# Column sums of the conditioning weights in four strips, on a fused two-layer encoder kernel

## The reference

```
m = silu(c) @ ada_w[layer, sub] + ada_b[layer, sub]        # 2048 x 6144 weights
shift, scale, gate = split(m, 3)
h = x * (1 + scale) + shift
x = layer_norm(ALPHA * x + (1 + gate) * sublayer(h))
```

## Time and profile before

| | |
|---|---|
| median of three runs | 2767.97 us (2763.74 to 2770.62) |
| profiled execution | 2772.19 us |
| its span | 2770.4 us |
| TensorE busy | 2607.1 us, 94% |
| VectorE busy | 1879.7 us, 68% |
| ScalarE busy | 1204.8 us, 43% |
| granted clock of TensorE, mean | 0.972 |
| data moved | 635 MB, 229 GB/s |

### The profile page before, as it was taken

The page is one execution under the profiler, slowest core; times in us unless marked ns, Lnnn a source line. Parts: engine busy times, 40 slices in busy tenths (PEclk is TensorE's granted clock), DMA queues, the critical chain, the costliest instruction groups (busy, mean ns, idle before and its releaser), DMA issues.

```text
span 2770.4 us, 43302 instructions
## 1 busy us (share of the span) xinstructions
PE 2607.1 (94%) x17220; PEld 2083.4 (75%) x17220; DVE 1879.7 (68%) x1946; ACT 1204.8 (43%) x1036; POOL 107.3 (4%) x154
## 2 busy tenths in 40 slices
PE   6989999977898999999999987699999999999998
PEld 2348888834586888888888862388778888888886
DVE  6876656668856776777777769767756666555555
ACT  4463333345535333343444455743443334344444
POOL 1012000000002000000000011000020000000000
PEclk9999999999999999999999988899999999999999
DMA  8898888822544887887878848778657777455552
GB/s 250 337 328 283 282 263 281 290 66 77 184 152 141 271 285 260 286 273 273 277 268 282 285 166 168 274 242 285 233 174 231 238 237 238 171 183 194 176 189 76
DMA packets 245356, 635.12 MB, mean 229 GB/s; under 512 B 33186, under 2 KB 34852, under 8 KB 240900
## 3 DMA queue, kind: packets, MB, share of 16 engines
q1 hardware_dynamic: 232548, 579.27, 63.0%
q0 software_dynamic: 9536, 34.48, 4.0%
q10 hardware_dynamic: 3168, 19.92, 1.8%
HBM read 613.83 MB, written 19.79 MB: 229 GB/s over the span
## 4 chain that ended last, share of the span: by engine, by line
PE 84%; DVE 7%; ACT 3%; DMA 3%; issue 2%; SPq 0%; DVEq 0%; ACTq 0%
PE PS L270 48%; PE PS L274 24%; PE PS L223 4%; DMA araw<-in_ada_w 2%; PE PS L444 1%; ACT Pb L1089 1%; PE PS L187 1%; PE PS L1011 1%; DVE wlo L260 1%; PE PS L712 1%; PE PS L985 1%; DMA acc<-in_ada_w 1%; PE PS L699 1%; ACT H L1089 1%; DVE X L1608 1%
## 5 line engine op out<-in xcount | busy, mean ns | idle before, releaser
L270 PE MATMUL PS<-H,whi 128*128 128x512 f32 x5888 | 1865.1, 398 | 27.0 <-DVE wlo L260 19.6
L260 DVE TENSOR_TENSOR wlo<-raw,whi 128x2048 fp32r<-128x2048 f32 x368 | 843.6, 2293 | 697.1 <-ACT whi L256 696.2
L274 PEld LDWEIGHTS PS<-H,wlo 128*128 128x128 f32 x5888 | 1113.4, 189 | 262.6
L256 ACT ACTIVATE whi<-raw 128x2048 fp32r<-128x2048 f32 x368 | 705.0, 1917 | 1225.8 <-PE PS L270 1210.2
L274 PE MATMUL PS<-H,wlo 128*128 128x256 f32 x5888 | 1162.2, 279 | 0.0
L270 PEld LDWEIGHTS PS<-H,whi 128*128 128x128 f32 x5888 | 904.2, 190 | 32.3 <-DVE wlo L260 26.0
L179 DVE SCALAR_TENSOR_TENSOR acc<-araw,cact,acc 128x1024 f32<-128x1024 f32 x240 | 307.6, 1282 | 1.4 <-DMA araw<-in_ada_w 1.0
L1089 ACT ACTIVATE Pb<-PS 128x1024 f32 (+5 forms) x106 | 106.4, 1010 | 91.7 <-PE PS L712 52.1
L1652 DVE TENSOR_TENSOR H<-Pb,H 128x512 fp32r<-128x512 f32 x128 | 87.7, 685 | 0.0
L1089 ACT ACTIVATE H<-Pb 128x512 fp32r (+2 forms) x131 | 82.3, 628 | 6.2 <-DVEq L1930 6.2
L1537 DVE TENSOR_TENSOR raw<-Pb,HF 128x1024 f32<-128x1024 f32 x64 | 74.1, 1221 | 12.0 <-DMA omat<-WF 9.4
(11 more groups left out here) (299 smaller groups left out, 1381.0 us busy)
## 6 DMA issues: line engine op xcount, KB each, us to landing
raw<-in_mlp_w SPq DMA_DIRECT2D x256, 1024.0 KB, 6.0
araw<-in_ada_w SPq DMA_DIRECT2D x274, 512.0 KB, 4.6
raw<-in_mix_w_in SPq DMA_DIRECT2D x64, 1024.0 KB, 7.7
raw<-in_s_w_glu SPq DMA_DIRECT2D x32, 1024.0 KB, 7.3
acc<-in_ada_w SPq DMA_DIRECT2D x40, 512.0 KB, 8.2
raw<-in_ada_w POOLq DMA_DIRECT2D x32, 512.0 KB, 4.1
raw<-in_mix_w_out SPq DMA_DIRECT2D x16, 1024.0 KB, 5.1
vmat<-Pb ACTq DMA_DIRECT2D x8, 1024.0 KB, 7.4
```

Of the source, the lines that this page charges most:

```text
L256: nc.scalar.activation(whi[:, s % 2, :], raw[:, s, :], ACT.Copy).then_inc(S("hi_done"), 1)
L260: nc.vector.tensor_tensor(wlo[:, s % 2, :], raw[:, s, :], whi[:, s % 2, :].bitcast(F), ALU.subtract).then_inc(S("lo_done"), 1)
L270: return nc.tensor.matmul(PS[:, b, :], w, H2[:, :, k, :], start=first, stop=last, skip_group_check=True)
L274: return nc.tensor.matmul(PS[:, b, 0:T], w, H2[:, 0, k, :], start=False, stop=last, skip_group_check=True)
```

## The change

For the four units SHIFT1, GATE1, SHIFT2 and GATE3 the sum is made in three steps. `ada_strips` on TensorE, where `ada_sum` stood: four products with 32 columns of ones as weights and 512 columns of `u.acc`, each into another quarter of the bank's partitions. `ada_copy` on ScalarE copies the bank, 128 x 512, over the first 512 columns of `u.acc`. `ada_turn` on TensorE turns these in four transposes into the same bank, and `ada_finish` picks 16 of the 512 columns. In a wide stage the turn stands ahead of tile 0 of slab 0 of the next block, and the copy behind ScalarE's split of that block's first slab. In a down stage the turn stands ahead of tile 3 of the first slab, behind the wait for the copy-out, and the copy behind the copy-out of the last up block. VectorE's program keeps its order; its wait in `ada_finish` is now for the turn. The other four units keep `ada_sum`.

```diff
@@ class Unit
             self.acc = acc[:, 2048 * half:2048 * half + 2048]
+            self.strip = 0
@@
+    for n, u in enumerate((SHIFT1, GATE1, SHIFT2, GATE3)):
+        u.strip = n + 1
@@
+    def ada_strips(pe, u, b):
+
+        pe.wait_ge(S("ada_used"), u.base + 32 + PRIME_ADA)
+        for j in range(4):
+            last = nc.tensor.matmul(PS[32 * j:32 * j + 32, b, :], ones[:, 0:32], u.acc[:, 512 * j:512 * j + 512],
+                                    start=True, stop=True, skip_group_check=True)
+        last.then_inc(S("ada_strips"), 1)
+
+    def ada_copy(act, u, b):
+
+        act.wait_ge(S("ada_strips"), u.strip)
+        nc.scalar.activation(u.acc[:, 0:512], PS[:, b, :], ACT.Copy).then_inc(S("ada_copied"), 1)
+
+    def ada_turn(pe, u, b):
+
+        pe.wait_ge(S("ada_copied"), u.strip)
+        for x in range(4):
+            last = nc.tensor.transpose(PS[:, b, x * P:(x + 1) * P], u.acc[:, x * P:(x + 1) * P], ident[:])
+        last.then_inc(S("ada_summed"), 1)
@@ def ada_finish(v, link, u, b):
-        link(nc.vector.tensor_tensor(MOD[:, u.sub, ms], PS[:, b, 0:16], ADAB[u.sub][:, ms], ALU.add))
+        if u.strip:
+            mod, bias = (z.rearrange("p (j x) -> p j x", x=4) for z in (MOD[:, u.sub, ms], ADAB[u.sub][:, ms]))
+            sums = PS[:, b, :].rearrange("p (x j r) -> p j x r", x=4, j=4)[:, :, :, 0]
+            link(nc.vector.tensor_tensor(mod, sums, bias, ALU.add))
+        else:
+            link(nc.vector.tensor_tensor(MOD[:, u.sub, ms], PS[:, b, 0:16], ADAB[u.sub][:, ms], ALU.add))
@@ def wide_products
                 pe.wait_ge(S("evac_done"), before)
-                ada_sum(pe, sums, 7)
+                ada_strips(pe, sums, 7)
@@
             for m in range(4):
+                if freed and s == 0 and m == 0:
+                    ada_turn(pe, freed, 7)
@@ def run_sum
-                ada_sum(pe, s.ada[0], b)
+                ada_strips(pe, s.ada[0], b)
@@ def down_slab
                             pe.wait_ge(S("evac_done"), evacs)
+                            if freed:
+                                ada_turn(pe, freed, 0)
@@ ScalarE, wide blocks, behind split_hi
+                            if s.sums and isinstance(blk, int) and blk == 1 and sl == 0:
+                                ada_copy(act, s.sums, 7)
@@ ScalarE, down_hi
                             evac(*prev, 1)
+                            ada_copy(act, prev[0].ada[0], 0)
```

## The result

| | before | after |
|---|---|---|
| median of six runs | 2767.22 us | 2750.27 us |
| range | 2763.74 to 2775.28 | 2750.05 to 2757.76 |
| profiled execution, its span | 2772.19, 2770.4 us | 2750.22, 2748.4 us |
| TensorE busy | 2607.1 us | 2591.7 us |
| granted clock, mean | 0.972 | 0.976 |

The ratio is 0.9942, with a 95% interval of 0.9924 to 0.9959: 16 us faster, between 11 and 21 (the two medians themselves differ by 17). The forecast was 15.05 us and 2752.9.

What follows compares the result with a forecast made beforehand. TensorE was taken to set the pace in the dense stages. Old sums 22.15 us; after, 4 x (1.1 + 0.5) + 0.6 + 0.1 = 7.1; gain 15.05, from a median of 2767.97 to 2752.9 us, range 2748 to 2761.

Steps and rivals of the forecast that it cites:

- The cost of the old form: Four one-column sums in dense stages: 2 x 5.15 + 5.12 + 6.73 = 22.15 us of the path, clock included.
- Strips: TensorE, each of four places: four overlapping 512-column products take 1.1 us, between 0.91 and 1.29.
- Turn: TensorE, each of four places: four transposes take 0.5 us, at least 0.4 and at most 0.7.
- The clock: TensorE's granted clock stays 1.00 over strips and turn, with no fall at any of the four places.
- rivals 1 and 2: Four places: clock falls once, gain 8.2, chance 0.13; or twice, gain 1.4 to 11.3 slower, chance 0.04 slower, 0.04 within.
- The copy: ScalarE: 0.60 us, hidden in wide stages; in down stages the next split starts 0.6 to 0.8 us later, also hidden.
- The moved wait: VectorE waits for the turn; wide stages: no stall, 1.2 us to spare, then 0.5 at the next slab.
- the stalls in the down stages: TensorE waits for VectorE's low part as the sum's cover goes: 0.6 us at SHIFT2, 0.1 at GATE3.
- Rival 3: Four strips run one after another, 3.64 us instead of 1.1; gain 5.6 with 0.7 of stalls covered, 2762.4; chance 0.08.
- rival 4: Wide places: VectorE's late multiply-add makes the slab behind it late, 2 us at each; gain 11, 2757; chance 0.09.
- T + 4.9: Wide stages, T the end of slab 3: VectorE's next low part ends then; TensorE wants it at T + 6.1.

Runs made afterwards that it cites:

- e5_half_sum: Kernel before with only 8 of the 16 one-column products at each of the four places, second half of the sums lost; one run 2751.95 us.
- e3_one_quarter: Full change with all four strip products sent to the first quarter of the partitions, so they can't overlap; one run 2767.2 us.
- e4: Full change with the four transposes of a turn issued eight times over; one run 2776.26 us.
- e7: Full change with VectorE's first multiply of SCALE2 moved ahead of its wait for the copied-out block in layer 0's down stage; one run 2753.55 us.
- e6_late_turn: Full change with the turn ahead of tile 3 instead of tile 0 of the next slab in the two wide stages; one run 2763.08 us.

## Why the prediction was right

- The cost of the old form, 22.15 us with the clock's part, was read from one execution; a mean over eight places gives 22.0. The step that carried the forecast was to read slabs by ScalarE's starts: by the chain alone, the four sums are 15.0 us, and the gain would have been forecast 7 us too small. That just one place in four was dear in the execution that was read is luck: with none or two, the same reading would have come out some 1.6 us lower or higher. e5_half_sum shows that the clock's part is a thing of its own.
- Strips, 1.1 us: measured 1.06 as a span, and 1.20 in slab 3 (6.77 - 5.57). Turn, 0.5: measured 0.45 in slab 0. Together 1.65 for 1.6. Choosing near the layer norm's row and scaling it by less than two was right; e3_one_quarter shows what the other reading would have cost.
- The clock, 1.00 at all four places: right, and rivals 1 and 2 did not come. e3 and e4 show it for pieces of 3.6 us too.
- The copy is hidden in the wide stages (ScalarE still waits 4.37 us for TensorE behind it) and delays the split in the down stages without effect: at SHIFT2 that split ends at 1238.65, and VectorE comes to the low part at 1240.06, straight behind its multiply. e7 takes 0.74 of the stall's 0.94 us away with the copy in place.
- The moved wait costs nothing in the wide stages. The spare time was about 1.5 us, forecast 1.2. e6_late_turn overdraws it and loses 2.9 and 4.6 us.
- The term of the sum that was mis-sized is the stalls in the down stages: forecast 0.6 and 0.1, measured 6.51 - 5.57 = 0.94 and 5.95 - 5.57 = 0.38. That the shorter sum uncovers them was right, and the chain on VectorE ended where the prediction put it: 1250.83 - 1243.20 = 7.63 us behind the start of the copy-out. VectorE and TensorE after, at SHIFT2; VectorE and TensorE's weight loads at GATE3:

```profile
1242.26 0.68 DVE L1687 TENSOR_TENSOR H<-Pb,H 128x512 fp32r<-128x512 f32 x1
...
1243.09 0.47 PE L298 MATMUL PS<-H,whi 128*128 128x512 f32 x1 [0.69 <-DVE H L1687]
```

```profile
2363.31 0.68 DVE L1687 TENSOR_TENSOR H<-Pb,H 128x512 fp32r<-128x512 f32 x1
...
2364.11 0.19 PEld L298 LDWEIGHTS PS<-H,whi 128*128 128x128 f32 x1 [0.44 <-issue]
```

At SHIFT2 the copy-out starts at 1235.31 and the chain ends at 1242.94, 7.63 us behind. The product behind it starts 0.15 later, 0.69 us after the one before has ended; in an undisturbed slab the two overlap. At GATE3 the low part ends at 2363.99, just as TensorE ends the slab; the weights of the next product, usually loaded early, are loaded only then, and 0.38 us go. So data that come just as they are wanted are late here. This is the likely reason why both stalls are 0.3 us above their forecast; no run varies it. Sum of places after: 7.9 us, forecast 7.1.
- Rival 3 (no overlap) and rival 4 (a slab late) did not come in the full change. Both mechanisms exist: e3 and e6 bring them about. But rival 3 counts 0.7 us of stalls as covered by the longer strips, and in e3 they stayed.
- Two small slips do not touch the sum. SHIFT1's sum ran 3.61 us, so what it cost beyond that is 5.16 - 3.61 = 1.55 and not 1.7. And from T + 4.9 the addition, the square and the multiply-add by their rows end at T + 8.6, not T + 8.8, which leaves 0.7 us to spare instead of 0.5.

So the forecast of 15.05 stands against 14.1 to 14.3 by the places and 16 by the times; the two differ by less than what the rest of the kernel varies. By the places the forecast is 0.8 too high, 0.6 of it the stalls. It did not foresee the 2 us by which the times exceed the places, and they are not shown to come from the change.

## What to carry to other kernels

Cost a small piece of work in a dense stream by the distance between two events of another engine that follows the stream, not by its own duration: here 5.1 to 6.7 us against 3.5 for most, because sixteen one-column products in a row lowered the clock for what came after. The same sum with the data streaming (512 columns) and the ones as weights in four quarters took 1.06 us, 1.65 with the turn, and left the clock at 1.00. When such a piece is shortened or moved, list what is queued behind each wait, since the old piece was also cover: 1.3 of some 15 us came back as stalls, and a turn set three tiles later gave back 7.5.

## What the runs showed of the hardware that was not expected

- Eight one-column products with 128 columns of weights (1.84 us) left the granted clock at 1.00; sixteen (3.5 us) lowered it to between 0.50 and 0.64 over the next 3 to 5 us at all eight places. At two of the eight it fell 0.9 us or more before they had ended (those two took 4.50 and 3.87 us, the others 3.46 to 3.61), which cost 1.4 to 1.6 us more.
- Eight records of 512-column products with 32 columns of weights, one after another in the same quarter for 3.62 us, left it at 1.00, and so did 32 float32 transposes in a row, 3.66 us.
- In e6, 1.97 us of idling of TensorE in a dense stage was followed by 0.65 over the next 4 us; at SHIFT1 of the same run 1.99 us of idling left it at 1.00.
